# Sparse-attention logits of the second token tile: one fp32 product exchanged for three fp32r passes

## What is computed

```python
def dsa_attention(q, ckv, iq, ik, iw, kv_norm_g, ik_norm_g, w_uv):
    q = q.reshape(b, s, DSA_HEADS, DSA_LATENT)          # 8 heads, 256 latent channels
    c = rmsnorm(ckv, kv_norm_g)
    ...
    vals, idx = lax.top_k(isc, topk)                    # 64 keys per token, by an indexer
    c_sel = jax.vmap(lambda cb, ib: cb[ib])(c, idx)
    logits = jnp.einsum('bqhc,bqkc->bqhk', qb, c_sel).astype(jnp.float32) * (DSA_LATENT ** -0.5)
    p = jax.nn.softmax(jnp.where(valid[:, :, None, :], logits, -jnp.inf), axis=-1)
    ob = jnp.einsum('bqhk,bqkc->bqhc', p.astype(c.dtype), c_sel)
    return jnp.einsum('bqhc,hcv->bqhv', ob, w_uv)
```

## Time and profile before

| | us |
|---|---|
| median of 3 executions (lowest, highest) | 1094.7 (1094.49, 1095.58) |
| the profiled execution | 1095.71 |
| its span, first to last instruction | 1094.0 |
| PE busy, share of the span | 1083.3, 99% |
| DVE busy | 794.4, 73% |
| ACT busy | 536.4, 49% |
| POOL busy | 27.2, 2% |
| mean granted clock of TensorE | 0.999 |

### The profile page before, as it was taken

The page is one execution under the profiler, slowest core; times in us unless marked ns, Lnnn a source line. Parts: engine busy times, 40 slices in busy tenths (PEclk is TensorE's granted clock), DMA queues, the critical chain, the costliest instruction groups (busy, mean ns, idle before and its releaser), DMA issues.

```text
span 1094.0 us, 14575 instructions
## 1 busy us (share of the span) xinstructions
PE 1083.3 (99%) x5057; PEld 898.5 (82%) x5057; DVE 794.4 (73%) x1385; ACT 536.4 (49%) x744; POOL 27.2 (2%) x45
## 2 busy tenths in 40 slices
PE   8999999999999999999999999999999999999997
PEld 7898888888887888889887778888888888888886
DVE  5555566688878887778957777878788777777445
ACT  5664444555555555545455444454444444436442
POOL 0000000000000001111100000000000000000000
PEclk9999999999999999999999999999999999999999
DMA  8776666565666646657665555654655567765552
GB/s 276 199 226 193 193 193 193 174 188 174 192 174 178 182 145 192 201 173 217 198 182 178 173 164 183 210 174 133 197 172 170 145 219 256 235 195 183 194 194 109
DMA packets 114120, 205.82 MB, mean 188 GB/s; under 512 B 11228, under 2 KB 18456, under 8 KB 113688
## 3 DMA queue, kind: packets, MB, share of 16 engines
q1 hardware_dynamic: 114032, 205.21, 61.4%
q10 hardware_dynamic: 40, 0.01, 0.0%
HBM read 203.10 MB, written 2.10 MB: 188 GB/s over the span
## 4 chain that ended last, share of the span: by engine, by line
PE 95%; DVE 4%; ACT 1%; issue 0%; DMA 0%; DVEq 0%; ACTq 0%
PE stream L1476 29%; PE stream L1478 29%; PE stream L1477 29%; PE stream L1597 2%; DVE wlo L875 1%; PE mixer L1722 1%; PE stream L1598 1%; DVE mixed L866 1%; DVE area L1114 0%; ACT whi L562 0%; PE mixer L1738 0%; PE mixer L1689 0%; PE mixer L1511 0%; PE mixer L1688 0%; PE mixer L1575 0%
## 5 line engine op out<-in xcount | busy, mean ns | idle before, releaser
L562 ACT ACTIVATE whi<-raw 128x1024 fp32r<-128x1024 f32 (+1 forms) x376 | 395.4, 1054 | 519.4 <-PE stream L1478 484.6
L875 DVE TENSOR_TENSOR wlo<-raw,whi 128x1024 fp32r<-128x1024 f32 (+1 forms) x376 | 456.6, 1218 | 260.8 <-ACT whi L562 257.6
L1476 PE MATMUL stream<-whi,xboth 128*128 128x512 f32 (+1 forms) x1248 | 491.1, 394 | 0.4 <-DVE wlo L875 0.3
L1478 PE MATMUL stream<-whi,xboth 128*128 128x512 f32 (+1 forms) x1248 | 484.3, 388 | 0.0
L1477 PE MATMUL stream<-wlo,xboth 128*128 128x512 f32 (+1 forms) x1248 | 483.8, 388 | 0.0
L1476 PEld LDWEIGHTS stream<-whi,xboth 128*128 128x128 f32 x1248 | 234.6, 188 | 51.7 <-issue 5.3
L1478 PEld LDWEIGHTS stream<-whi,xboth 128*128 128x128 f32 x1248 | 234.5, 188 | 48.8
L1477 PEld LDWEIGHTS stream<-wlo,xboth 128*128 128x128 f32 x1248 | 234.8, 188 | 45.9
L1476 PE MATMUL stream<-whi,yhi 128*128 128x512 f32 x192 | 76.6, 399 | 0.2 <-DVE ylo L1318 0.2
L1478 PE MATMUL stream<-whi,ylo 128*128 128x512 f32 x192 | 74.9, 390 | 0.0
L1477 PE MATMUL stream<-wlo,yhi 128*128 128x512 f32 x192 | 74.8, 390 | 0.0
(11 more groups left out here) (241 smaller groups left out, 560.8 us busy)
## 6 DMA issues: line engine op xcount, KB each, us to landing
raw<-in_w_in SPq DMA_DIRECT2D x286, 512.0 KB, 3.7
raw<-in_w_branch SPq DMA_DIRECT2D x48, 512.0 KB, 4.6
raw<-in_w_out SPq DMA_DIRECT2D x32, 512.0 KB, 3.7
raw<-in_w_in SPq DMA_DIRECT2D x12, 256.0 KB, 3.3
mixed<-in_x SPq DMA_DIRECT2D x8, 256.0 KB, 6.8
area<-in_x SPq DMA_DIRECT2D x2, 1024.0 KB, 7.7
out<-area SPq DMA_DIRECT2D x8, 256.0 KB, 2.3
raw<-in_dsa_w_uv SPq DMA_DIRECT2D x4, 256.0 KB, 2.9
```

The costliest lines, as they stand in the source:

```text
L562: nc.scalar.activation(whi[:, slot, :, 0:width], raw[:, slot, :, 0:width], ACT.Copy).then_inc(whi_ready, 1)
L875: nc.vector.tensor_tensor(wlo[:, slot, :, 0:width], raw[:, slot, :, 0:width], whi[:, slot, :, 0:width].bitcast(F32), ALU.subtract).then_in ...
L1476: nc.tensor.matmul(to, left_hi[:, kt, tokens], high, start=first, stop=False)
L1478: last = nc.tensor.matmul(to, left_lo[:, kt, tokens], high, start=False, stop=final)
```

## The change

For the second token tile the two fp32 matmuls are replaced, for each half of the channels, by three fp32r matmuls: query high by key high, query high by key low, query low by key high. The first tile stays in fp32. The query's two parts are made per head: ACT rounds `dsa_qT[:, :, P:]` into `dsa_qhi` (128x256) and DVE subtracts it into `dsa_qlo` (128x256). Both stand at u = 0 of the head, ahead of that step's rounding (ACT) and split (DVE). PE waits for `dsa_qlo_ready` between the first tile's and the second tile's matmuls.

```diff
@@ block.scalar, stage PP[1]
                 for v in range(PAIR_UNITS):
-                    round_unit(PP[1], i, v)
                     s, u = v // 6, v % 6
                     h = i * 2 + s
+                    if u == 0:
+                        act.wait_ge(dsa_turned, h + 1)
+                        nc.scalar.activation(dsa_qhi[:, :, :], dsa_qT[:, :, P:], ACT.Copy).then_inc(dsa_qhi_ready, 1)
+                    round_unit(PP[1], i, v)
@@ block.vector, stage PP[1]
                 for v in range(PAIR_UNITS):
-                    split_unit(PP[1], i, v)
                     s, u = v // 6, v % 6
                     h = i * 2 + s
+                    if u == 0:
+                        dve.wait_ge(dsa_qhi_ready, h + 1)
+                        nc.vector.tensor_tensor(dsa_qlo[:, :, :], dsa_qT[:, :, P:], dsa_qhi[:, :, :].bitcast(F32),
+                                                ALU.subtract).then_inc(dsa_qlo_ready, 1)
+                    split_unit(PP[1], i, v)
@@ block.tensor, stage PP[1], u == 1
                         pe.wait_ge(dsa_turned, h + 1)
-                        for t, a, n in ((0, 0, P), (1, P, 2 * P)):
-                            for c in range(2):
-                                last = nc.tensor.matmul(M[1][:, a:a + n], dsa_qT[:, c, t * P:(t + 1) * P],
-                                                        cT[:, c, 0:n], start=(c == 0), stop=(c == 1))
+                        for c in range(2):
+                            nc.tensor.matmul(M[1][:, 0:P], dsa_qT[:, c, 0:P], cT[:, c, 0:P],
+                                             start=(c == 0), stop=(c == 1))
+                        pe.wait_ge(dsa_qlo_ready, h + 1)
+                        for c in range(2):
+                            to = M[1][:, P:3 * P]
+                            nc.tensor.matmul(to, dsa_qhi[:, c, :], chi[:, c, :], start=(c == 0), stop=False)
+                            nc.tensor.matmul(to, dsa_qhi[:, c, :], clo[:, c, :], start=False, stop=False)
+                            last = nc.tensor.matmul(to, dsa_qlo[:, c, :], chi[:, c, :], start=False, stop=(c == 1))
```

More of the change, by code:

```diff
@@ L176, in build @@
         clo = sb("clo", [P, 2, SEQ], F32R)
+        dsa_qhi = sb("dsa_qhi", [P, 2, P], F32R)
+        dsa_qlo = sb("dsa_qlo", [P, 2, P], F32R)
         mixed = sb("mixed", [P, TILES, D_MODEL])
@@ L352, in build @@
         dsa_turned = sem("dsa_turned")
+        dsa_qhi_ready, dsa_qlo_ready = sem("dsa_qhi_ready"), sem("dsa_qlo_ready")
         dsa_logits, dsa_negmax, dsa_exp = sem("dsa_logits"), sem("dsa_negmax"), sem("dsa_exp")
```

## The result

| | before | changed |
|---|---|---|
| median of 4 executions (lowest, highest), us | 1095.12 (1094.49, 1095.58) | 1103.77 (1103.29, 1105.54) |
| the profiled execution, us | 1095.71 | 1105.54 |
| its span, us | 1094.0 | 1103.8 |
| granted clock of TensorE, mean | 0.999 | 0.993 |

The ratio is 1.0082, with a 95% interval from 1.007 to 1.0094. The sign and the place were as forecast; the size was 2 us more. What was missed shows in the last row of the table.

The account below looks back on a forecast made before the run. PE was taken to bound the kernel, almost without waits. Cheaper passes -1.4, even-head stalls +6.8 and odd-head stalls +1.2 made +6.6 us on 1094.7, so 1101.3 us, with a range of 1098.8 to 1105.6.

Parts of the forecast that it names:

- What bounds the kernel: In the stage changed, PE sets the end with almost no wait: each us it computes less or waits counts fully.
- The passes: Second tile on PE: six fp32r matmuls at 0.115 us, 0.69, replace 0.87 us; gain 0.18 per head, 1.4 for eight.
- Even heads: Heads 2, 4, 6: dsa_qlo queues behind DVE's gate_branch, so PE stands 2.26 us before the second tile; 6.8 us in all.
- The price of the row: PE's restart after a DVE wait elsewhere in the trace, 0.34 us, as upper end; 0.2 was taken.
- Odd heads: Heads 1, 3, 5, 7: the parts follow the last query transposes, so PE stands 0.29 us before the second tile; 1.2 us.
- Head 0: First head: dsa_qlo is ready at 720.64, before PE comes at 721.89, so nothing waits.
- What is queued behind: ACT's rounding and DVE's split behind the new instructions slip, but PE has 3.6 us to spare in an even head; costs nothing.
- the sum's silence on the clock: The sum over the stage, -1.4 + 6.8 + 1.2 = +6.6 us, had no term for a falling PE clock.
- Stall and clock: Forecast stall at 84%; rival at 5%: PE at half pace about 8 us after each of three gaps, 4 us each, 1113 us.
- a stall only once: Rival: the first even-head stall puts PE 2.3 us behind and later heads find dsa_qlo ready; +2.1, 1096.8 us; 4%.
- The wait that doesn't bind: Rival: dsa_qlo is ready before PE reaches the second tile, leaving only the cheaper passes; -1.4 us, 1093.3; 4%.
- the dear passes: Rival: second-tile fp32r matmuls cost 0.217 us each, like fp32 records; +3.4 in place of -1.4, 1106.1 us; 3%.

Follow-up runs that it names:

- half gap: The changed kernel with the low part between the two pairs of gate_branch instructions, in even heads but 0: 1097.71 us against 1095.00 before the change, ratio 1.0025.
- the second series: The changed kernel measured once more with nothing edited, against the kernel before: 1105.50 us (1103.53 to 1106.52), ratio 1.0098.

## Why the prediction came out as it did

- **What bounds the kernel** was right: every step of PE went into the time. Kernels without falls of the clock time at their steps: +2.7 measured for +2.7 (half gap), +2.3 for +2.2, +0.8 for +0.5, -1.1 and -1.25 for -1.4.
- **The passes** were right: 0.12 us each for the 0.115 forecast, 0.17 us gained per head for 0.18. They lie nearer to the cheap end than to the 0.145 of the earlier trace rows. The rule of the Trainium skill ("TensorE: Matmul & The Clock Gate", "Back-to-back issue gap") has 0.109 for 256 columns; the trace is dearer again, as for 344.
- **Even heads**: the gap was forecast at 2.26 us and was 2.2. The low part took 0.41 us for 0.43, and PE restarted 0.16 us behind its end (760.65 to 760.81) for 0.2. The price of the row, with two instructions more in it, was rightly kept as the upper end.
- **Odd heads**: the gap was forecast at 0.29 and was 0.26, the step +0.09 for +0.11. **Head 0** waits for nothing, -0.17 for -0.18.
- **What is queued behind** was right as far as it went: no unit came late. But only the splits were followed. That nothing else on DVE cost time was in part luck: the maxima and the exponentials behind them had only 0.24 us to spare, and the stall covered them. Moving the low part ahead of `gate_branch` laid that bare.
- **The step that failed is the sum's silence on the clock.** The steps without it make -0.2 + 0.4 + 6.1 = +6.3, the forecast's 6.6 within 0.3. The rest of the 8.7, some 2.4 us, is what one or two falls at 1.58 us cost, and the second series, at +10.5, has room for two or three; the two profiled executions had three and one. Stall and clock stood as two cases that exclude each other, 84% and 5%, while a fall is an addition to the stall and comes behind some of the gaps. Its price was put at 4 us per gap from the length of the opening, which says how long PE took to come up from the start and not how long it stays down behind a short gap; the rows show 3 us at 0.50 and 1.58 us lost. One of the prediction's own signs of being wrong came true with it: matmuls of 0.63 us behind the gaps.
- **Luck.** The range, 1098.8 to 1105.6, was said to leave the clock out. Its upper part was meant for dear terms, none of which came, and the falls went into it: 1103.8 us in the first series, 1105.5 in the second, at the very edge.
- **The other rivals**: a stall only once is refuted, the three gaps are equal within 0.01 us. The wait that doesn't bind and the dear passes are refuted by the rows above.

How many falls an execution has can't be read from its time alone, since the opening moves it by up to 1.3 us; the mean granted clock gives an estimate. In the profiled executions gaps of 1.0 us had no fall in three, gaps of 2.2 us five in nine, and gaps of 3.35 us three in three, though by the mean clocks not in each of the other executions. What decides whether a given gap brings a fall stays open.

## What to carry to other kernels

A wait that is put into the engine that sets the time must be priced at the releaser's place in its own queue, behind what stands there in every case of the loop: here an instruction of 0.4 us stood behind 2.4 us of work in three heads out of eight, and cost 6 us where the arithmetic that it served gained 1.4. Make the operands one unit earlier than they are wanted. Then follow what that pushes back, through to the next wait of the engine that sets the time: the next smallest slack (0.24 us here) stays hidden until the first stall is gone. And a gap of about 2 us in a stream of matmuls costs its length and sometimes a stretch at half clock on top.

## What the runs showed of the hardware

- TensorE's granted clock fell from 1.00 to 0.50 behind a gap of 2.2 us in which PE stood still, in the first case 0.9 us after PE had resumed, and came back while PE worked on; matmuls of 512 columns were 0.43 us apart in it. In the profiled executions it did so behind five of nine such gaps, with none of three of 1.0 us, and with three of three of 3.35 us, where it fell inside the gap and cost more (2.7 to 2.8 us in place of 1.6). With the gap filled by transposes it didn't.
- fp32r matmuls of 256 columns follow each other at 0.12 us, two plain fp32 ones of 128x256 take 0.87. Six passes in place of two such products were worth 0.17 us per head, a fifth of the 0.87, where the parts cost nothing.
- A waiting PE starts its next matmul about 0.16 us after the end of the DVE instruction that it waited for.
